# A sparse attention whose selection is added by VectorE instead of TensorE, with the steps' work on TensorE in another order

## The reference

```
score = einsum('bqhs,bqh->bqs', relu(iq . ik), iw)      # one index score per query and key, 16 index heads
score = where(key <= query, score, -inf)
_, idx = top_k(score, 128)                              # the same 128 keys for all heads
logits = (q . k[idx]) * scale + rel_bias[bucket(query - idx)]   # 16 heads of width 64, one shared k and v
p = softmax(where(idx <= query, logits, -inf))
o = p . v[idx]
out = silu(d_gate) * o
```

## Time and profile before

| | us |
|---|---|
| median of 3 runs | 2930.26 |
| lowest, highest | 2928.46, 2931.2 |
| the profiled execution, its own time | 2931.68 |
| its span, from the first to the last instruction | 2929.8 |

### The profile page before, as it was taken

The page is one execution under the profiler, slowest core; times in us unless marked ns, Lnnn a source line. Parts: engine busy times, 40 slices in busy tenths (PEclk is TensorE's granted clock), DMA queues, the critical chain, the costliest instruction groups (busy, mean ns, idle before and its releaser), DMA issues.

```text
span 2929.8 us, 34587 instructions
## 1 busy us (share of the span) xinstructions
PE 2823.2 (96%) x14062; PEld 2176.6 (74%) x14062; DVE 1116.1 (38%) x1848; ACT 959.2 (33%) x1479; POOL 1077.7 (37%) x529
## 2 busy tenths in 40 slices
PE   5979999989999998899999999999999999999999
PEld 3557788878778874478887677766787877777787
DVE  4164323142322143322212468744223455566411
ACT  4222332242233221332222312365322223666411
POOL 1253213213321330135543343444455343545443
PEclk9989999999999999999999999999999999999999
DMA  8844412213575231413433233322443333322442
GB/s 324 298 154 124 136 58 72 72 26 101 172 180 115 62 83 43 129 36 112 122 90 87 72 101 87 101 71 74 148 122 104 100 87 94 87 76 78 138 123 83
DMA packets 456605, 318.28 MB, mean 109 GB/s; under 512 B 32352, under 2 KB 404960, under 8 KB 455680
## 3 DMA queue, kind: packets, MB, share of 16 engines
q1 hardware_dynamic: 424400, 280.09, 32.9%
q10 hardware_dynamic: 32048, 35.98, 4.8%
HBM read 299.14 MB, written 28.95 MB: 112 GB/s over the span
## 4 chain that ended last, share of the span: by engine, by line
PE 92%; DVE 3%; DMA 2%; ACT 1%; issue 1%; POOL 1%; SPq 0%; ACTq 0%; DVEq 0%; POOLq 0%
PE acc L1863 77%; PE aux L1863 8%; PE ssq L1866 3%; PE ssq L1863 3%; DMA raw<-in_w_in 1%; PE aux L1866 1%; POOL w_lo L1180 1%; DVE rstd L1417 1%; DVE x_t L1361 0%; PE acc L1866 0%; DVE x_t L1359 0%; DMA dist_mask_sb<-in_dist_mask 0%; DVE h_lo L1369 0%; ACT w_hi L862 0%; DVE p L1489 0%
## 5 line engine op out<-in xcount | busy, mean ns | idle before, releaser
L1180 POOL TENSOR_TENSOR w_lo<-raw,w_hi 128x1024 fp32r<-128x1024 f32 x362 | 868.7, 2400 | 1698.8 <-ACT w_hi L862 1698.6
L1863 PE MATMUL acc<-h_hi,w_hi 128*128 128x512 f32 (+1 forms) x3232 | 1214.0, 393 | 33.6 <-DVE gate_raw L1379 19.7
L1863 PE MATMUL acc<-h_hi,w_lo 128*128 128x512 f32 (+1 forms) x3232 | 1172.2, 380 | 0.0
L1863 PE MATMUL acc<-h_lo,w_hi 128*128 128x512 f32 (+1 forms) x2464 | 872.7, 376 | 0.0
L862 ACT ACTIVATE w_hi<-raw 128x1024 fp32r<-128x1024 f32 x362 | 383.0, 1059 | 1171.0 <-PE acc L1863 1077.0
L1863 PEld LDWEIGHTS acc<-h_hi,w_hi 128*128 128x128 f32 x3232 | 585.0, 188 | 206.9 <-issue 77.2
L1863 PEld LDWEIGHTS acc<-h_hi,w_lo 128*128 128x128 f32 x3232 | 583.6, 188 | 119.4
L1863 PEld LDWEIGHTS acc<-h_lo,w_hi 128*128 128x128 f32 x2464 | 440.9, 189 | 91.1 <-issue 10.6
L1863 PE MATMUL acc<-out_t_lo,w_hi 128*128 128x512 f32 x768 | 299.0, 389 | 0.0
L1417 DVE RECIPROCAL rstd<-rstd 128x512 f32<-128x512 f32 (+1 forms) x29 | 118.0, 4070 | 352.8 <-ACT rstd L906 352.7
L1863 PEld LDWEIGHTS acc<-out_t_lo,w_hi 128*128 128x128 f32 x768 | 144.3, 188 | 29.0
(11 more groups left out here) (235 smaller groups left out, 2337.2 us busy)
## 6 DMA issues: line engine op xcount, KB each, us to landing
raw<-in_w_in SPq DMA_DIRECT2D x52, 1024.0 KB, 5.9
raw<-in_even_w_in SPq DMA_DIRECT2D x41, 1024.0 KB, 5.6
raw<-in_odd_w_in SPq DMA_DIRECT2D x36, 1024.0 KB, 5.6
ada_ring<-in_w_ada SPq DMA_DIRECT2D x32, 1024.0 KB, 5.5
gate_ring<-in_w_ada SPq DMA_DIRECT2D x16, 1024.0 KB, 7.0
raw<-in_w_out SPq DMA_DIRECT2D x16, 1024.0 KB, 5.9
raw<-in_even_w_out SPq DMA_DIRECT2D x16, 1024.0 KB, 5.9
raw<-in_odd_w_out SPq DMA_DIRECT2D x16, 1024.0 KB, 6.5
```

The lines of the kernel that those rows point to most:

```text
L1180: G_.tensor_tensor(WL[half][:], RAW[G.rs][:, half * HALF * P:(half + 1) * HALF * P], WH[half][:].bitcast(F32), ALU.subtract).then_inc(S["l ...
L1863: return M.matmul(out_, lhsT, rhs, start=start, stop=stop, skip_group_check=True)
```

## The change

The selection is no longer a product on TensorE. Scores go to `AUX` in place of `ACC[:, half, 512:]`, alone. For steps B, C and D VectorE adds the mask to them in one instruction for both heads (new line 1639, called the *pick* here), from PSUM and SBUF into `P2` in SBUF. It signals `d_picked`, for which VectorE itself waits. The fused maximum then reads `P2` instead of PSUM; in step A it reads PSUM as before. The identity `IDR` and the instruction that made it (line 1762) go, and `SEL` is plain float32.

Since `AUX` now holds scores, outputs go to `ACC[:, u % 2, 512:]`. On TensorE a step is now scores (s), outputs (s-4), turns (s-3); on VectorE it is reciprocal (s-1), pick and maximum (s), gating (s-4), copy (s-3).

```diff
-    V2, IDR = at("v2_nat", QT * 64, 172 * K1), at("ident_r", P, 173 * K1, F32R)
+    V2 = at("v2_nat", QT * 64, 172 * K1)
-    SEL = at("select_mask", 3 * SEQ, 178 * K1, F32R)
+    SEL = at("select_mask", 3 * SEQ, 178 * K1)
...
@@ VectorE, dsa(s)
+                if s < 32:
+                    j, qt = DSA_UNITS[s]
+                    nk = P * (qt + 1)
+                    need(dve, "d_turned", 2 * (s - 4) + 2)
+                    if qt:
+                        p = P2[qt][:].rearrange("p (h n) -> p h n", n=nk)
+                        sel = SEL[:, (qt - 1) * SEQ:(qt - 1) * SEQ + nk].unsqueeze(1).to_broadcast([P, 2, nk])
+                        dve.wait_ge(S["d_scored"], 2 * s + 2)
+                        Vv.tensor_tensor(p, AUX[:].rearrange("p (h n) -> p h n", n=512)[:, :, 0:nk], sel, ALU.add).then_inc(S["d_picked"], 1)
+                        dve.wait_ge(S["d_picked"], 3 * j + qt)
+                    for half in range(2):
+                        c, slot = 2 * (s % 8) + half, (2 * j + half) % 4
+                        dve.wait_ge(S[f"tb{slot}"], 16 * (j // 2 + 1))
+                        dve.wait_ge(S["d_scored"], 2 * s + half + 1)
+                        p = P2[qt][:, half * nk:half * nk + nk]
+                        Vv.tensor_tensor_reduce(out=p, in0=p if qt else AUX[:, half * 512:half * 512 + nk],
+                                                in1=TR[slot][:, SEQ - nk:SEQ], scale=-1.0, scalar=-NEG, op0=ALU.add,
+                                                op1=ALU.min, accum_out=LNG[:, c:c + 1]).then_inc(S["d_max"], 1)
                 if s >= 4:
...
-                    Vv.tensor_tensor(o, AUX[:, (u % 2) * 512:(u % 2) * 512 + P], o, ALU.mult).then_inc(S["d_fin"], 1)
-                if s < 32:
...
+                    Vv.tensor_tensor(o, ACC[:, u % 2, 512:512 + P], o, ALU.mult).then_inc(S["d_fin"], 1)
...
@@ VectorE, after the group of kind ikw
-                        L.done(Vv.tensor_copy(IDR[:], IDENT[:]))
...
@@ TensorE, dsa(s): the scores now stand ahead of the outputs
-                    if qt:
-                        pe.wait_ge(S["sel_done"], 1)
-                        for half in range(2):
-                            mm(ACC[:, half, 512:512 + nk], IDR[:], SEL[:, (qt - 1) * SEQ:(qt - 1) * SEQ + nk], True, False)
...
-                        mm(ACC[:, half, 512:512 + nk], Q2[rows, j * SEQ + qt * P:j * SEQ + (qt + 1) * P], K2[rows, 0:nk],
-                           qt == 0, True).then_inc(S["d_scored"], 1)
+                        mm(AUX[:, half * 512:half * 512 + nk], Q2[rows, j * SEQ + qt * P:j * SEQ + (qt + 1) * P], K2[rows, 0:nk],
+                           True, True).then_inc(S["d_scored"], 1)
```

More of the change, by code:

```diff
@@ L516, in build @@
             "i_scored", "i_relu", "i_acc",
-            "d_scored", "d_max", "d_exp", "d_inv", "d_norm", "d_turned", "d_pt0", "d_pt1", "d_out", "d_fin",
+            "d_scored", "d_picked", "d_max", "d_exp", "d_inv", "d_norm", "d_turned", "d_pt0", "d_pt1", "d_out", "d_fin",
             "w_scored", "w_max", "w_exp", "w_inv", "w_norm", "w_turned", "w_pt0", "w_pt1", "w_out", "w_fin")}
@@ L1636, in dsa @@
                     dve.wait_ge(S["d_out"], u + 1)
-                    Vv.tensor_tensor(o, AUX[:, (u % 2) * 512:(u % 2) * 512 + P], o, ALU.mult).then_inc(S["d_fin"], 1)
-                if s < 32:
-                    j, qt = DSA_UNITS[s]
-                    nk = P * (qt + 1)
-                    need(dve, "d_turned", 2 * (s - 4) + 2)
-                    for half in range(2):
[L1643 to L1648, removed]
+                    Vv.tensor_tensor(o, ACC[:, u % 2, 512:512 + P], o, ALU.mult).then_inc(S["d_fin"], 1)
                 if 3 <= s < 35:
@@ L2126, in dsa @@
             def dsa(s):
+                if s < 32:
+                    j, qt = DSA_UNITS[s]
+                    nk = P * (qt + 1)
+                    pe.wait_ge(S["normed"], 2 + j)
+                    need(pe, "d_max", 2 * s)
+                    if s == 0:
+                        pe.wait_ge(S["y_copied"], 2)
+                    for half in range(2):
+                        rows = slice(64 * half, 64 * half + 64)
+                        mm(AUX[:, half * 512:half * 512 + nk], Q2[rows, j * SEQ + qt * P:j * SEQ + (qt + 1) * P], K2[rows, 0:nk],
+                           True, True).then_inc(S["d_scored"], 1)
                 if s >= 4:
@@ L2135, in dsa @@
                         for half in range(2):
-                            e = mm(AUX[64 * half:64 * half + 64, (u % 2) * 512:(u % 2) * 512 + P], V2[:, b * 64:b * 64 + 64],
+                            e = mm(ACC[64 * half:64 * half + 64, u % 2, 512:512 + P], V2[:, b * 64:b * 64 + 64],
                                    PT2[:, half * 512 + b * P:half * 512 + (b + 1) * P], b == 0, b == qt)
                     e.then_inc(S["d_out"], 1)
[L2139 to L2145, removed]
-                    if qt:
-                        pe.wait_ge(S["sel_done"], 1)
-                        for half in range(2):
-                            mm(ACC[:, half, 512:512 + nk], IDR[:], SEL[:, (qt - 1) * SEQ:(qt - 1) * SEQ + nk], True, False)
-                    for half in range(2):
-                        rows = slice(64 * half, 64 * half + 64)
-                        mm(ACC[:, half, 512:512 + nk], Q2[rows, j * SEQ + qt * P:j * SEQ + (qt + 1) * P], K2[rows, 0:nk],
-                           qt == 0, True).then_inc(S["d_scored"], 1)
                 if 3 <= s < 35:
```

## The result

| | median us | lowest to highest | runs |
|---|---|---|---|
| before | 2931.09 | 2928.22 to 2934.10 | 18 |
| changed | 2936.88 | 2933.99 to 2939.63 | 18 |

The ratio is 1.002, with a 95% interval of 1.0013 to 1.0028: 5.8 us slower. The forecast was 2934.3 (+4.0), with most of the chance on a change too small to be told from none. The time lies in the forecast's own range of 2931 to 2938. The loss is small, but the interval leaves out 1, so it is a loss.

A forecast was written before the change was run, and what follows sets the result against it. TensorE, 92% of the chain, was taken to bound the kernel. Gains of 18.2 us against new waits of 22.2 gave +4.0: 2935.7 profiled, 2934.3 median; own range 2931 to 2938, whole range 2922 to 2940.

The forecast's parts named there:

- The port: VectorE maxima of B, C, D with two SBUF inputs stand still until GpSimd's running instruction ends, up to 2.37 us.
- the prediction's zero: Start of an attention group, its first main matmul on TensorE; step D's scores were to begin at -2.44 us.
- the first rival: Fused maxima in SBUF are exempt from the port's lock: about -8 us, 2922; chance 0.13.
- the second: Rival: a step's two maxima go through together, GpSimd's normalisation behind both: about -5 us, 2925; chance 0.09.
- The loop through A, B and C: D's late maximum delays later steps; TensorE waits 1.0 us at A, 0.07 at B, 1.33 at C per group.
- Waits in sum: New TensorE waits: 7.0 us at A, 0.5 at B, 9.3 plus 2.5 at C, 2.9 in the tail; 22.2 in all.
- the tail: Behind the last group TensorE waits for two VectorE copies, 2.0 us and then 0.9, 2.9 together.
- C's first group: Wait at step C in the first group: present 1.35 us, pick 0.7, earlier TensorE 0.43, so 2.5.
- The gain on TensorE: Selection removed from steps B, C and D: 1.64 us a group, 13.1 for eight groups.
- Selection worth less: Rival: each small-matmul phase has a fixed start that stays with the scores, 5 of 13 us stay: +9, 2939; chance 0.08.
- Slower chain: Rival: VectorE loses more at each port lock or own-engine wait; at 0.3 us more, +10, 2940; chance 0.10.
- the cast: Instruction that made the identity, 0.59 us; removing it was to start the first index scores 0.5 us sooner.

The follow-up runs named there:

- e1: Changed kernel, but the pick writes its sum back to PSUM and the fused maxima read PSUM and SBUF: 2923.14 us, ratio 0.9974 to the kernel before.
- e5: Changed kernel with the pick written to PSUM and the low part made behind step C: 2914.07 us, ratio 0.9945 to the kernel before.
- e8: Changed kernel with pick in PSUM, low part behind step C, and the old order in a step: 2913.89 us, ratio 0.9943 to the kernel before.
- e4: Changed kernel, but VectorE makes the output tile's low part behind step C, not ahead of step B: 2926.05 us, ratio 0.9986 to the kernel before.
- e6: Kernel before, with only the low part moved behind step C: 2927.58 us, ratio 0.9987 to the kernel before.
- e3b: Changed kernel with the old order in a step (outputs before scores, gating before pick and maxima): 2937.41 us, ratio 1.0025 to the kernel before.
- e10: e5 plus four unread products on TensorE during its long wait ahead of step B's first scores: 2914.13 us, ratio 0.9946 to the kernel before.

## Why the prediction was right, and where its sizes were off

**The port.** Right. Counted from the start of D's scores (2.44 ahead of the prediction's zero), the first maximum was to end at 4.09, the normalisation at 5.49 and the second maximum at 6.09. Measured, from 1971.93: 4.24, 5.57 and 6.12. The form isn't exempt (1811 ns against 689, and e1 takes it away), so the first rival falls. The normalisation lies between the maxima, so the second falls too. The picks took 0.66, 0.96 and 1.23, for a forecast of 0.70, 0.96 and 1.23.

**The loop through A, B and C.** Right in kind and nearly in size. A: forecast 1.0 in each of seven groups, measured 1.00 in six and 2.03 in the first of them, where step D has no outputs yet and is 1.03 shorter on TensorE (1.57 for 2.60), so that TensorE is at A that much sooner. B: forecast 0.07, measured 0.18 to 0.20 in six and none in the first. C: forecast 1.33, measured 1.17 to 1.31 in six and 1.03 in the first of the seven. A group takes 22.26 (from D's scores at 1971.93 to the next at 1994.19), forecast 22.05. Nearly all of the 0.2 lies between A's scores and B's, 4.39 us for a forecast of 4.22: B's wait is 0.11 longer, since the reciprocal of step A began 9.87 from D's scores and not 9.74.

**Waits in sum.** 20.7 us at A (8.0), B (1.1), C (9.6) and the tail (2.0), and the 2.06 of the first group, which was there before as 2.02 behind the first unit. The prediction had 22.2 (7.0, 0.5, 11.8, 2.9). C's first group gave 0.88 instead of 2.5, because TensorE came there late itself, at half clock. The tail's second wait of 0.9 didn't come, for the same reason: TensorE was 1.7 late there by its clock.

**The gain on TensorE.** The removed work was sized rightly, but the clock, a loss behind long waits, was left out. 13.1 us of busy time were to go; 8.9 went. From the main matmul ahead of step D to the one behind it TensorE took 3.26 us before and 2.60 in the changed kernel, so the selection itself is gone in full. What came in its place is mostly the clock. In the changed kernel it was at 0.50 from 1897.5 to 1900.5 with a part on either side, and from 2068.0 to 2071.0 likewise. Summed over half-microsecond windows that is 1.7 us lost at each, 3.4 of the 4.2. Before had no such stretch. The last 0.8 fits the way in which a wait is counted. Without a wait, the scores start 0.32 us behind the start of the last main matmul; ahead of a wait, all 0.39 of that matmul count as busy. So each wait adds 0.07 of busy time, and the stretch has 23 waits where it had 9: an estimate of 1.0. The same count gives 13.1 - 1.7 + 0.5 = 11.9 for e5, with two waits and one fall of the clock; measured are 176.36 - 164.29 = 12.1.

**Rivals left.** "Selection worth less" (+9) falls with e5, where 16.6 of the 18.2 us can be had, and with e8, where the steps are shorter by 1.63 a group: no fixed start stays with the scores. "Slower chain" (+10) was right in its direction, a group does take 0.2 more, but its size would have needed more at every restart. In the profiled executions the difference is 6.1, 2.1 above the forecast: waits 1.3 less (16.3, where the prediction's terms give 22.2 - 4.6), work 4.2 more, and the stretch 0.8 earlier than the cast explains. The three partly cancel, so that the total is this near is in part luck; the path by which the waits came is not.

## What to carry to other kernels

When work moves from a full engine to an idle one, ask first which operands the moved work leaves for the next instruction: here the intermediate in SBUF made the next VectorE instruction wait for GpSimd and cost some 13.5 us, and writing it back to PSUM, at the same price, made the change a gain. An instruction that is blocked is harmless or costly by what is queued behind it and when the bounding engine asks for that, so place it right behind a deadline and not ahead of one (e4 and e6). A wait on TensorE can cost more than its length: behind several of the 2-us waits here the clock fell and took 1.7 us more.

## What the hardware showed that was not expected

TensorE's granted clock falls to 0.50 (1.2 GHz) shortly after some waits of about 2 us, with matmuls running again, and comes back after some 3.5 us. In the changed kernel, the wait of the tail and what follows, on TensorE's timeline:

```profile
2067.59 0.54 PE L1869 MATMUL acc<-p_t,v_nat 128*64 128x128 f32 x4 [2.04 <-issue]
2068.06 1.11 PE L1872 MATMUL ssq<-ident_sb,p 128*128 128x128 f32 x4
...
2069.82 0.63 PE L1869 MATMUL acc<-h_hi,w_lo 128*128 128x512 f32 x1
2070.25 0.63 PE L1869 MATMUL acc<-h_hi,w_hi 128*128 128x512 f32 x1
2070.68 0.63 PE L1869 MATMUL acc<-out_t_lo,w_hi 128*128 128x512 f32 x1
2071.10 0.44 PE L1869 MATMUL acc<-h_hi,w_lo 128*128 128x512 f32 x1
2071.39 0.39 PE L1869 MATMUL acc<-h_hi,w_hi 128*128 128x512 f32 x1
```

Main matmuls start every 0.43 us and then every 0.23 again; it costs about 1.7 us each time. In the stretch studied it followed the first group's wait (2.01 to 2.06) in the changed kernel and in seven of the nine experiments, the tail's 2.04 in the changed kernel and in e4, and in e3b the waits of 2.48 and 2.23. It did not follow that first wait in the kernel before (2.02) and in e3b (2.06), nor the 2.03 at A in the changed kernel and in e4, nor any wait of 1.82 or less. In sum, 12 of 16 waits of 2.0 us and more were followed by half clock, and no stretch at half clock came here without such a wait. In e10, where TensorE worked through the wait, the clock stayed up, in one profiled execution. What decides between falling and not for waits of one length remains open.

Also new: when VectorE and GpSimd both have work queued whose inputs are all in SBUF, each of GpSimd's instructions can look longer (1.92 for 1.47) by the end of VectorE's, and VectorE's by the whole of GpSimd's (1.94 for 0.69). The same section of the Trainium skill ("SBUF — State Buffer", "Who interferes with whom") says that the order of issue decides who blocks; these rows agree, each engine waited for the one that had begun.
